# Two high products and then two low ones in the common matmul step of a two-block transformer kernel

## What is computed

```python
# first block
h = rms_norm(x) ; q, k, v, c_b, c_c, c_x, g_a, g_c = split(h @ w_in)      # 2048 -> 10240
y_attn = attention(rms_norm(q), rms_norm(k), v) @ w_attn_out               # 8 heads of 128
y_conv = (c_b * causal_conv3(c_c * c_x)) @ w_conv_out
r = x + (sigmoid(g_a) * y_attn + sigmoid(g_c) * y_conv) @ w_o
r = r + square(relu(rms_norm(r) @ w_up)) @ w_down                          # 2048 -> 8192 -> 2048
r = r + sigmoid(rms_norm(r) @ w_ple_gate) * (p @ w_ple_proj)
# second block, with 16 meta tokens ahead
h = concat(meta, r)
a, g = split(rms_norm(h) @ conv_w_in + b) ; u = causal_conv31(a * sigmoid(g)) + b
h = h + rms_norm(silu(layer_norm(u)) @ conv_w_out + b)
h = h + rms_norm((silu(n @ w_gate) * (n @ w_up)) @ w_down), n = rms_norm(h)   # 2048 -> 5632 -> 2048
return h[16:]
```

## Time and profile before

| | |
|---|---|
| three runs | 2543.49, 2543.50, 2542.21 us; median 2543.49 |
| span of the profiled execution | 2542.0 us |
| its time apart from the span | not given |
| TensorE matmul busy | 2523.6 us (99%), 14605 matmuls |
| TensorE weight load busy | 2224.7 us (88%), 14605 loads |
| VectorE, ScalarE, GpSimd busy | 1722.5, 1252.9, 431.3 us |
| mean granted clock of TensorE | 0.998 |
| DMA | 466.38 MB, mean 183 GB/s |
| the chain that ended last | TensorE 90%, VectorE 8% |

### The profile page before, as it was taken

One profiled execution on the slowest core, in us unless ns is written; L12 is line 12 of the kernel. 1 busy time (PEld: TensorE's weight loads), 2 busy tenths in 40 slices (PEclk: granted clock), 3 DMA queues, 4 the chain that ended last, 5 costly groups with the idle time before them and its releaser, 6 DMA issues.

```text
span 2542.0 us, 42618 instructions
## 1 busy us (share of the span) xinstructions
PE 2523.6 (99%) x14605; PEld 2224.7 (88%) x14605; DVE 1722.5 (68%) x2097; ACT 1252.9 (49%) x1554; POOL 431.3 (17%) x291
## 2 busy tenths in 40 slices
PE   9999999999999999999999999999999999999998
PEld 8888888888888888888888899988888888888887
DVE  6568875587665665665667889985766556654665
ACT  6456555554544444444444554555644444444443
POOL 0034410002100000000002368973400000000001
PEclk9999999999999999999999999999999999999999
DMA  7655565665556666656565566536466656556554
GB/s 235 185 168 180 165 189 181 197 194 178 188 183 192 187 188 189 189 190 189 183 193 185 183 171 170 166 109 206 150 197 200 195 177 198 185 191 187 183 182 163
DMA packets 470962, 466.38 MB, mean 183 GB/s; under 512 B 14522, under 2 KB 441012, under 8 KB 470708
## 3 DMA queue, kind: packets, MB, share of 16 engines
q1 hardware_dynamic: 470336, 464.97, 59.1%
q10 hardware_dynamic: 546, 0.38, 0.1%
HBM read 463.20 MB, written 2.10 MB: 183 GB/s over the span
## 4 chain that ended last, share of the span: by engine, by line
PE 90%; DVE 8%; issue 1%; ACT 1%; POOL 0%; DMA 0%; DVEq 0%; POOLq 0%; ACTq 0%
PE gp L450 49%; PE gp L453 22%; DVE xp L1839 6%; PE gp L818 3%; PE gp L816 3%; PE gp L817 3%; PE gp L459 3%; PE gp L488 1%; PE gp L630 1%; PE gp L631 1%; PE gp L490 1%; PE gp L632 1%; PE xp L777 0%; DVE gp L1804 0%; DVE wlo L1423 0%
## 5 line engine op out<-in xcount | busy, mean ns | idle before, releaser
L1423 DVE TENSOR_TENSOR wlo<-stage,whi 128x1024 fp32r<-128x1024 f32 x809 | 1010.0, 1263 | 676.3 <-ACT whi L879 670.7
L879 ACT ACTIVATE whi<-stage 128x1024 fp32r<-128x1024 f32 x874 | 914.1, 1057 | 929.0 <-PE gp L453 601.7
L450 PE MATMUL gp<-A,whi 128*128 128x512 f32 x3968 | 1320.5, 393 | 0.3 <-DVE A L1530 0.3
L453 PE MATMUL gp<-A,wlo 128*128 128x256 f32 x3264 | 915.1, 280 | 0.0
L450 PEld LDWEIGHTS gp<-A,whi 128*128 128x128 f32 x3968 | 739.1, 188 | 164.1 <-DVE A L1530 0.7
L453 PEld LDWEIGHTS gp<-A,wlo 128*128 128x128 f32 x3264 | 614.5, 188 | 0.0
L450 PE MATMUL gp<-B,whi 128*128 128x512 f32 x1536 | 536.3, 394 | 0.6 <-issue 0.6
L453 PE MATMUL gp<-B,wlo 128*128 128x256 f32 x1536 | 430.5, 280 | 0.0
L450 PEld LDWEIGHTS gp<-B,whi 128*128 128x128 f32 x1536 | 287.7, 187 | 66.8 <-issue 1.0
L453 PEld LDWEIGHTS gp<-B,wlo 128*128 128x128 f32 x1536 | 290.2, 189 | 0.0
L2144 POOL TENSOR_TENSOR sq<-r 128x512 f32 x24 | 29.5, 1228 | 795.7 <-DVE r L1733 757.9
(11 more groups left out here) (324 smaller groups left out, 2143.5 us busy)
## 6 DMA issues: line engine op xcount, KB each, us to landing
stage<-in_w_in SPq DMA_DIRECT2D x160, 512.0 KB, 4.1
stage<-in_w_up SPq DMA_DIRECT2D x128, 512.0 KB, 3.8
stage<-in_w_down SPq DMA_DIRECT2D x128, 512.0 KB, 3.6
stage<-in_ffn_w_gate SPq DMA_DIRECT2D x88, 512.0 KB, 4.5
stage<-in_ffn_w_up SPq DMA_DIRECT2D x88, 512.0 KB, 4.4
stage<-in_ffn_w_down SPq DMA_DIRECT2D x88, 512.0 KB, 4.5
stage<-in_conv_w_in SPq DMA_DIRECT2D x64, 512.0 KB, 4.1
stage<-in_w_o SPq DMA_DIRECT2D x32, 512.0 KB, 4.4
```

Of the source, the lines that this page charges most:

```text
L450: nc.tensor.matmul(bank.rearrange("p (a t) -> p a t", a=2), hi, both_parts(M, kt), start=first, stop=False)
L453: done = nc.tensor.matmul(bank[:, T:2 * T], lo, M[:, kt, 0:T], start=False, stop=last)
L879: nc.scalar.activation(unit_homes(n, slot)[0], stage[:, slot, :], ACT.Copy).then_inc(hi_ready, 1)
L1423: nc.vector.tensor_tensor(lo, stage[:, slot, :], hi.bitcast(F32), ALU.subtract).then_inc(lo_ready, 1)
```

## The change

In the common branch of `step` the four matmuls of each k are taken in another order. Before: high and low of column tile 0, then high and low of column tile 1. After: high of tile 0, high of tile 1, low of tile 0, low of tile 1. The branch `hi_first` stays as it is, and so do `side_by_side`, conv2, the v panels and the last products.

```diff
                         for m in range(2):
                             c = k * HPW + m * P
-                            hi, lo = whi[:, slot, c:c + P], wlo[:, slot, c:c + P]
                             bank = gp[:, 2 * j + m, :]
-                            nc.tensor.matmul(bank.rearrange("p (a t) -> p a t", a=2), hi, both_parts(M, kt),
+                            nc.tensor.matmul(bank.rearrange("p (a t) -> p a t", a=2), whi[:, slot, c:c + P], both_parts(M, kt),
                                              start=first, stop=False)
-                            if not hi_first:
-                                done = nc.tensor.matmul(bank[:, T:2 * T], lo, M[:, kt, 0:T], start=False, stop=last)
+                        if not hi_first:
+                            for m in range(2):
+                                c = k * HPW + m * P
+                                done = nc.tensor.matmul(gp[:, 2 * j + m, T:2 * T], wlo[:, slot, c:c + P], M[:, kt, 0:T],
+                                                        start=False, stop=last)
```

## The result

The changed kernel takes 2551.67 us (median of five runs, 2551.47 to 2552.80) beside 2543.50 us of the kernel before (2542.21 to 2543.67 in the same comparison). The ratio is 1.0035 [1.0024, 1.0046]: slower by a third of a per cent, which a measurement of this kernel can tell from no change. The span of the profiled execution grew from 2542.0 to 2549.7 us, by 7.7.

What follows compares the result with a forecast made beforehand. TensorE's matmul starts were taken as the bound, with weights early. The profiled span 2542.0 us, plus 0 for the change, plus 1.5 around the span, gave 2543.5 us; range 2535 to 2552.

Steps and rivals of the forecast that it cites:

- the unchanged waits: Common step: waits for the low buffer and the moving data stay where they were; put at nothing.
- the buffer hand-over: End of each weight buffer: the last low matmul still alone hands it back, so other engines see no change; nothing.
- the evacuation: Accumulators: evacuation still waits for the unit's last matmul, so the first tile's later low product goes unseen; nothing.
- the carrying over from the high-first units: Common step: starts spaced as in high-first steps on A, 0.694 us a k against 0.697; change put at 0.
- The term put at 0 for A: The 408 common-step units (one weight buffer, 16 matmuls each) with moving data from A: no change in time.
- All at the longest seen on their own operand: Upper bound over all 600 common-step units: 7.2 us on B plus 3.8 on A, 11.0 us more.
- rival 1's small form: Long units of gate, first up round, glu1 and glu2 fall back to short: 4.9 us less, 2538.6; within same's 0.68.
- rival 2: Attn_out, conv_out, later three up rounds: B's 131 short units turn long, 7.2 us more, 2550.7 to 2554.5; chance 0.16.
- Rival 3: TensorE: changing bank every matmul causes pauses and lowers the granted clock; one unit in twenty costs 84 us, 2627; chance 0.01.
- the signs that the prediction named: Profile after: starts 0.23, 0.23, 0.12, 0.12; units 2.78 to 2.79 us in down rounds, 2.77 in later up rounds; full clock.
- error in the root: Common step: prediction wrong at root if any kind of start moves more than some ns with the clock full.

Runs made afterwards that it cites:

- eight and eight: Common step runs a unit's eight high matmuls, then its eight low ones; beside the kernel before: 2542.99 us, ratio 0.9999 [0.9990, 1.0009].

## Why the prediction was wrong

**The bound was read rightly.** TensorE's starts set the time, the clock stayed full and the waits of TensorE stayed the same. The steps that cost the unchanged waits, the buffer hand-over and the evacuation at nothing hold: outside the 600 units of the common step the trace differs by 0.7 us in all, and that is less, not more.

**The step that failed** is the carrying over from the high-first units: "A k of the new order is then 2 x 0.231 + 2 x 0.116 = 0.694 us". On A a k of after takes 2.813 / 4 = 0.703. The two new neighbours, high after high and low after low, do each occur in the earlier trace rows, but the distance from a matmul to the next is not a property of these two alone. As means over the units on A that nothing interrupts, the steps high to high, high to low, low to low and low to high take 234.1, 230.8, 119.1 and 119.2 ns in after, and 232.1, 229.3, 116.5 and 118.3 in eight and eight on the same A: no one neighbour carries the loss, all four are 1 to 3 ns longer. The term put at 0 for A measured +8.9 us; the lengths read from the rows give much the same, 296 x 0.026 + 112 x 0.013 = 9.2. Eight and eight shows that the reading of the earlier trace rows was right for what it was: a common step in the very order of these rows does cost nothing on A. It was the wrong order to read.

**The bound for A failed with it.** "All at the longest seen on their own operand" took 2.800 from the earlier trace rows as the longest length of A and allowed 3.8 us for it. The longest of an old order is no bound for a new one: A went to 2.813 everywhere, also in glu1 and glu2.

**For B the sum came out near 0 by luck.** Two changes that the forecast did not have cancel. The long length of gate and of the first up round is gone, as in rival 1's small form, but to 2.787 and not to 2.772: 61 x (2.827 - 2.787) = 2.4 us less. The 131 short units lost, as rival 2 said, but 0.015 each and not 0.055: 2.0 us more. Together that is -0.4, beside the measured -0.6.

**Rival 2 had nearly the right time for a wrong reason.** Its 2550.7 to 2554.5 holds the measured 2551.67, but its place was B, and its point against ("on A the order changes nothing") is the one that broke. The range held the time, at 0.3 us from its upper end, but by the price of a rival that did not happen, which is luck; the chance of 0.17 for slower was too small, because all the evidence for "no change" was one row pattern in another order.

**Rival 3 did not happen.** The granted clock is full in after's page, and eight and eight changes the bank with every matmul too, at a granted clock of 0.998, and loses nothing. What the Trainium skill, TensorE: Matmul & The Clock Gate, section "A second HAM failure mode: psum-queue depth-cycling", tells of another kernel, pauses and a swinging clock, shows in no run here.

**Of the signs that the prediction named, the lengths told and the starts hardly did.** The down rounds are at 2.813 and not at 2.78 to 2.79, the later up rounds at 2.787 and not at 2.77, and glu1 at 2.813 is in none of its cases. The sign for an error in the root was a start that moved by "more than some ns"; none moved by more than about 3 from the 0.231 and 0.116 of the earlier trace rows, and that was enough, since it falls on every k of 408 units. The neighbours do matter in a way that the high-first steps don't show. Shown by the runs: the loss is on A, it belongs to the order in pairs, and it goes when A's rows stand 512 columns apart in place of 544. Not shown: what in the chip makes it so.

## What to carry to other kernels

Where matmul starts are the bound, don't add up distances between two kinds of neighbours into a new order, which failed here: measure a whole period in that very order, with the same operands and the same layout, for a length seen in another order was neither a forecast nor a bound. Read the step between the rows of the moving data along with the order, since here one decided what the other cost. And run such a kernel several times before it is believed: the runs of two combinations of order and layout fell into two groups of times, and a single profile shows one of them.

## What was not expected of the hardware

- TensorE keeps one of a few lengths for the same 16 matmuls, from 2.773 to 2.827 us a unit (2%), with order and layout; on rows 512 apart two orders have both a short and a long one, and runs of one program differ by some 13 us (2543.37 to 2545.31 and 2556.35 to 2558.51). That the two lengths make this difference is likely, not shown.
- Where the weights stand against the rows moves single starts by up to 6 ns: 128 bytes between them exchange the patterns of even and odd k on A, and leave the sum at 2.813.
- 128 bytes between the buffers, with the program otherwise the same, moved the high-first units from 2.787 to 2.807 us and the last products by 6.6 us, and the kernel by 8.7 us in one run (2551.67 to 2560.41), more than the change studied here. The high-first units in after and with the weights shifted:

```profile
320.00 2.02 PE L449 MATMUL gp<-A,whi 128*128 128x512 f32 x8
...
331.14 2.02 PE L449 MATMUL gp<-A,whi 128*128 128x512 f32 x8
```

```profile
321.87 2.02 PE L450 MATMUL gp<-A,whi 128*128 128x512 f32 x8
...
333.10 2.02 PE L450 MATMUL gp<-A,whi 128*128 128x512 f32 x8
```

Four units take 11.14 us in the first and 11.23 in the second, 2.785 and 2.807 each; five units in the earlier trace rows gave 2.786.
